# Summing eight of the modulation chunks of a conditioned conformer block on VectorE in SBUF

## The chip, the cores and the metric

The kernel runs on one core of a Trainium2 chip. The metric is the device time of one execution in microseconds (us). Three runs of the kernel before took 1474.2, 1476.01 and 1476.91 us, so the time before is the median, 1476.01 us. The trace shows the engines of the core: TensorE (PE, with its weight loads as PEld), VectorE (DVE), ScalarE (ACT), GpSimd (POOL) and SyncE (SP), which issues all the transfers of this stretch.

## What is computed

Two transformer-like blocks over 256 tokens of width 1024 (fp32). Only the start of the first block matters here:

```python
c_act = silu(c)                                  # (1, 1024)
mod = c_act @ mod_w + mod_b                      # (1, 6144): six rows of 1024
sh_m, sc_m, gt_m, sh_f, sc_f, gt_f = split(mod, 6)
h = rmsnorm(x, norm_pre_mix) * (1 + sc_m) + sh_m
u = h @ a_pw1_w + a_pw1_b                        # 1024 -> 2048
a, gt = split(u, 2);  u = a * sigmoid(gt)
u = causal_dwconv(u, dw_w) + dw_b                # 31 taps along the tokens
u = silu(layernorm(u, ln_g, ln_b))
y = u @ a_pw2_w + a_pw2_b
x = x + gt_m * rmsnorm(y, norm_post_mix)
```

The modulation row `mod` is a product of one vector of 1024 with a matrix of 1024 x 6144. The matrix is read in 24 chunks of 256 columns, 1 MB each.

## The kernel before

Every engine has its own program, in a fixed order written out by hand, and the engines wait for each other on semaphores. Large fp32 products are made of three products of rounded parts: a chunk of weights is loaded by SP into `a_raw` (two buffers), ScalarE writes its rounded high part (`split_hi`, L121), VectorE the remainder (`split_lo`, L125, which reads `a_raw` and the high part and writes the low part), and TensorE multiplies (L140 to L142). `split_lo` of a chunk also frees its `a_raw` buffer for the next load.

The stretch of the change is the first projection (`a_pw1_w`), eight steps j = 0 to 7, each over 128 channels. In step j the engines do this, in this order:

- TensorE: `project(j)` (48 matmuls for each of two halves of the work, in all L140 to L142), then from step 1 on `mod_sum` of the chunks of one unit of the modulation (L600), `mean(j-2)` (L907), `convolve(j-1)` (L899), and `mod_post(unit)` (L625 or L631).
- ScalarE: `split_hi(j+1)` (L121), the sigmoid (L799), `mod_take` of the unit's chunks (L609), its four of the sixteen shift copies (L789), `conv_out(j-1)` (L758).
- VectorE: `split_lo(j+1)` (L125), the gated product u (L1050), its six shift copies (L1054), then `mod_columns` (L642 to L645) or `mod_gate` (L654, L655) of the unit.
- GpSimd: the tap matrices of this step (L739, a product of two SBUF tensors, 128x1024; from step 2 on it waits for `convolve(j-2)`), its six shift copies (L745, L746) once u is there, and in step 5, behind its shift copies, the remainder of `mem` (L750, a difference of two SBUF tensors, 128x2048).

`convolve(j)` needs the tap matrices and the shift copies of all three engines; `project(j)` needs `split_lo` of its chunk and u of step j-2.

One chunk of the modulation goes through three pieces. `mod_sum` multiplies the chunk with silu(c) on TensorE: eight matmuls of 128x256 on 32 columns of the array each, four side by side, so that four partial sums stand in PSUM (in the trace 16 matmul records for a chunk). `mod_take` copies them to `modp` (two buffers) on ScalarE. `mod_post` adds the four partial sums in a second matmul with `sel`, a matrix with ones in four rows. Steps 1 to 4 take two chunks each (units 4 to 7: chunks 8 and 9, 10 and 11, 12 and 13, 14 and 15), steps 5 to 7 one each (units 8 to 10: chunks 16, 17, 18), and behind step 7 comes chunk 19 (unit 11), with `mean(6)`, `convolve(7)` and `mod_post(11)` behind it, and then the product of `mem` with its weights. The four slots for chunks are loaded by SP, in its fixed order among the other weights; the load of chunk i waits for `mod_used` of chunk i - 4.

Of the kernel before, what the change touches and what calls it, by code (L numbers as in the profile page):

```python
# [23 lines left out]
ALU = mybir.AluOpType  # L24
# [3 lines left out]
P = 128  # L28
# [185 lines left out]
def build_program(nc, A, out):  # L214
    with ExitStack() as ctx:
# [3 lines left out]
        def sem(name):  # L219
            return ctx.enter_context(nc.semaphore(name))  # L220
# [319 lines left out]

        def first_block():

            mods, u_pad, taps_w, shifted, conv, sq, sig, rstd, modp, stat32, sel, mask32, ones_mean = carve(
                (MOD_SLOTS, ACH), (2, PAD + SEQ + 2), (2, QUAD * TAPS), (2 * 4, SHIFT_LEN), (KD, SEQ), (KD, SEQ),
                (2, SEQ), (SEQ,), (2, MOD_COLS), (KD, QUAD), (P,), (QUAD,), (P,))
            hT = sq
            yb = shifted.rearrange("p a n -> p (a n)")[:, 0:NT * D].rearrange("p (t d) -> p t d", t=NT)
            xn = conv.rearrange("p k t -> p (k t)").rearrange("p (t d) -> p t d", t=NT)
# [12 lines left out]
            mod_loaded = [sem(f"mod_loaded{s}") for s in range(MOD_SLOTS)]  # L561
            mod_used, mod_taken, mod_posted, post_read = (sem(n) for n in ("mod_used", "mod_taken", "mod_posted",
                                                                         "post_read"))
            cond_ready, cond_sig = sem("cond_ready"), sem("cond_sig")
            xn_done, xn_turned = sem("xn_done"), sem("xn_turned")
            affine_done, input_done = sem("affine_done"), sem("input_done")
# [16 lines left out]
            def mod_bank(i):  # L583
                return 2 + i % 2 if i < 8 else (6, 3)[i % 2] if i < 20 else 4 + i % 2

            def post_bank(u):
                return 1 if u < 4 else 7

            def load_mod(sp, i):
                if i >= MOD_SLOTS:  # L590
                    sp.wait_ge(mod_used, i - MOD_SLOTS + 1)
                sp.dma_start(mods[:, i % MOD_SLOTS], A["mod_w"][MOD_ORDER[i]]).then_inc(mod_loaded[i % MOD_SLOTS], 16)

            def mod_sum(pe, i):

                pe.wait_ge(mod_loaded[i % MOD_SLOTS], 16 * (i // MOD_SLOTS + 1))
                if i >= 2:
                    pe.wait_ge(mod_taken, i - 1)
                for k in range(KD):
                    ins = pe.matmul(ps[quad[k % 4], mod_bank(i), 0:MOD_COLS], stat32[:, k],  # L600
                                    mods[:, i % MOD_SLOTS, k * MOD_COLS:(k + 1) * MOD_COLS], start=k < 4, stop=k >= 4)
                ins.then_inc(mod_used, 1)

            def mod_take(act, i):

                act.wait_ge(mod_used, i + 1)
                if i >= 2:
                    act.wait_ge(mod_posted, (i - 2) // 2 + 1 if i < 18 else i - 9)
                act.activation(modp[:, i % 2], ps[:, mod_bank(i), 0:MOD_COLS], ACT.Copy).then_inc(mod_taken, 1)  # L609

            def mod_copy(dve, i):

                dve.wait_ge(mod_used, i + 1)
                dve.wait_ge(mod_posted, i - 9)
                dve.tensor_copy(modp[:, i % 2], ps[:, mod_bank(i), 0:MOD_COLS]).then_inc(mod_taken, 1)

            def mod_post(pe, u):

                pe.wait_ge(mod_taken, unit_chunks(u)[-1] + 1)
                if 0 < u < 12:  # L620
                    pe.wait_ge(post_read, u)
                for s, i in enumerate(unit_chunks(u)):
                    if u < 8:
                        for h in range(2):
                            ins = pe.matmul(ps[:, post_bank(u), MOD_COLS + 2 * s + h:MOD_COLS + 2 * s + h + 1],  # L625
                                            modp[:, i % 2, h * P:(h + 1) * P], sel[:, 0:1], start=True, stop=True)
                    else:
                        c = u - 12
                        out_ = ps[:, 7, MOD_COLS:512] if u < 12 else \
                            ps[:, 6 + c // 2, (c % 2) * MOD_COLS:(c % 2 + 1) * MOD_COLS]  # L630
                        ins = pe.matmul(out_, sel, modp[:, i % 2], start=True, stop=True)  # L631
                ins.then_inc(mod_posted, 1)

            def mod_columns(dve, u):
# [31 lines left out]
            with nc.Block() as block:  # L666
# [46 lines left out]
                @block.gpsimd  # L713
                def _(pool):
                    pool_steps.step(pool, pool.memset(ident[:], 0.0))
                    pool_steps.step(pool, pool.affine_select(out=ident[:], in_=ident[:], compare_op=ALU.not_equal, fill=1.0,
                                                             base=0, pattern=[[-1, P]], channel_multiplier=1))
                    for i, v in enumerate((RMS_EPS, LN_EPS, LNX_EPS, 4 * LN_EPS)):
                        pool_steps.step(pool, pool.memset(eps[:, i:i + 1], v))
                    pool_steps.step(pool, pool.memset(stat32, 0.0))  # L720
                    pool_steps.step(pool, pool.memset(sel, 0.0))
                    for q in range(4):
                        pool_steps.step(pool, pool.memset(sel[q * QUAD:q * QUAD + 1], 1.0))
                        pool_steps.step(pool, pool.tensor_copy(mask32[quad[q]], ident[quad[q], quad[q]]))
                    pool_steps.step(pool, pool.memset(u_pad[:, :, 0:PAD], 0.0))
                    pool_steps.step(pool, pool.memset(u_pad[:, :, PAD + SEQ:PAD + SEQ + 2], 0.0))
                    pool_steps.step(pool, pool.memset(ones_mean, 1.0 / D))
                    pool_steps.step(pool, pool.memset(x_all[:, :, D:], 0.0))
                    pool_steps.step(pool, pool.memset(rows_all[:, :, D:], 0.0))
                    pool_steps.step(pool, pool.memset(head_ones[:], 0.0))  # L730
                    for h in range(2):
                        pool_steps.step(pool, pool.memset(head_ones[h * HD:(h + 1) * HD, h * HD:(h + 1) * HD], 1.0))
                    constants_at.append(pool_steps.n)
                    pool.wait_ge(rest_loaded, 16)
                    for j in range(KD):
                        if j >= 2:
                            pool.wait_ge(conv_pe, j - 1)
                        weights = cols("a_dw_t", TAPS * KD)[:, j * TAPS:(j + 1) * TAPS]
                        pool.tensor_tensor(taps[j % 2], mask32.unsqueeze(1).to_broadcast([P, TAPS, QUAD]),  # L739
                                           weights.unsqueeze(2).to_broadcast([P, TAPS, QUAD]),  # L740
                                           ALU.mult).then_inc(taps_made, 1)
                        pool.wait_ge(u_done, j + 1)
                        pool.wait_ge(taps_made, j + 1)
                        for q, a in SHIFTS_BY["pool"][:-1]:
                            pool_steps.step(pool, pool.tensor_copy(*shift_views(j, q, a)))  # L745
                        pool.tensor_copy(*shift_views(j, *SHIFTS_BY["pool"][-1])).then_inc(shift_pool, 1)  # L746
                        pool.wait_ge(shift_pool, j + 1)
                        if j == 5:
                            pool.wait_ge(mem_hi, 1)
                            pool.tensor_tensor(mem_parts[:, 1], mem_raw, mem_parts[:, 0].bitcast(F32),  # L750
                                               ALU.subtract).then_inc(mem_lo, 1)
# [3 lines left out]
                def _(act):  # L755
# [37 lines left out]
                    for j in range(KD):  # L793
# [6 lines left out]
                                       bias=col("a_pw1_b", KD + j)).then_inc(sig_done, 1)  # L800
                        if j:
                            for i in unit_chunks(PAIR_STEPS.get(j, GATE_STEPS.get(j))):
                                mod_take(act, i)
                        shifts(j)
                        if j:
                            conv_out(j - 1)
                    mod_take(act, unit_chunks(11)[0])
                    ring_a.split_hi(act, g_mem + 1)
                    conv_out(KD - 1)
                    for k in range(KD):  # L810
# [68 lines left out]
                def _(pe):  # L879
# [46 lines left out]
                    for j in range(1, KD):  # L926
# [4 lines left out]
                        project(j, 1, range(KD)).then_inc(ring_a.used, 1)  # L931
                        unit = PAIR_STEPS.get(j, GATE_STEPS.get(j))
                        for i in unit_chunks(unit):
                            mod_sum(pe, i)
                        if j >= 2:
                            mean(j - 2)
                        convolve(j - 1)
                        mod_post(pe, unit)
                    mod_sum(pe, unit_chunks(11)[0])
                    mean(KD - 2)  # L940
                    convolve(KD - 1)
                    mod_post(pe, 11)
# [73 lines left out]
                def _(dve):  # L1016
# [27 lines left out]
                    dve.wait_ge(rest_loaded, 16)  # L1044
                    for j in range(KD):
                        ring_a.split_lo(dve, g_pw1 + j + 1)
                        dve.wait_ge(sig_done, j + 1)
                        if j >= 2:
                            dve.wait_ge(conv_pe, j - 1)
# [6 lines left out]
                        if j in PAIR_STEPS:  # L1056
                            mod_columns(dve, PAIR_STEPS[j])
                        elif j in GATE_STEPS:
                            mod_gate(dve, GATE_STEPS[j])
                    ring_a.split_lo(dve, g_mem + 1)  # L1060
                    mod_gate(dve, 11)
                    dve.wait_ge(mean_pe, 1)
# [1954 lines left out]
```

## Time and profile before

| what | value |
|---|---|
| median of three runs | 1476.01 us (1474.2 to 1476.91) |
| the profiled execution's own time | 1475.35 us |
| its span in the trace | 1473.3 us |
| PE busy in the span | 1426.6 us, 97% |
| DVE busy | 952.4 us, 65% |
| ACT busy | 684.5 us, 46% |
| POOL busy | 157.6 us, 11% |

The span is what the trace covers; the execution's own time holds 2.05 us more. The busy shares are means over the whole kernel, and the stretch of the change is about 90 us of it. Matmuls overlap each other in the records, so the distance from one start to the next tells more of TensorE's time than the length of one.

### The profile page before, as it was taken

The numbers are of one execution on the slowest core, as the hardware profiler recorded it, in microseconds if no ns is written. First come the engines' busy times: TensorE is split into PE (matmuls) and PEld (weight loads), VectorE is DVE, ScalarE is ACT, GpSimd is POOL, SyncE is SP. The second block draws the span as 40 slices with busy tenths as digits, with TensorE's granted clock in tenths as the row PEclk, the third lists the DMA queues.
The fourth block names the chain that finished last, engine by engine and source line by source line (L and its number), as shares of the span: only waits on it lengthen the run. The fifth ranks groups of instructions, "written<-read, shape, count | busy, mean of one in ns | idle before, by whom it ended". The sixth has DMA issues, their size and how long they took to land.

```text
span 1473.3 us, 31313 instructions
## 1 busy us (share of the span) xinstructions
PE 1426.6 (97%) x12734; PEld 1298.2 (88%) x12734; DVE 952.4 (65%) x1284; ACT 684.5 (46%) x875; POOL 157.6 (11%) x179
## 2 busy tenths in 40 slices
PE   5999989999999999999999999999999999999997
PEld 3877779999899998998878999999999999899996
DVE  2656776666755556596677655676566678865656
ACT  3444554545533345754445334353343466534332
POOL 1342022232000002103300000000000012000000
PEclk8899999999999999999999999999999999999999
DMA  9975456666566665430127666656666444576662
GB/s 364 320 270 201 143 172 186 192 178 199 159 196 182 185 179 150 144 115 32 32 61 208 182 186 192 195 162 200 191 180 188 140 144 144 157 216 198 185 184 88
DMA packets 297973, 257.75 MB, mean 175 GB/s; under 512 B 7072, under 2 KB 274336, under 8 KB 294816
## 3 DMA queue, kind: packets, MB, share of 16 engines
q1 hardware_dynamic: 297888, 256.49, 57.3%
q8 instruction: 68, 1.11, 0.3%
q14 instruction: 17, 0.14, 0.0%
HBM read 255.42 MB, written 1.05 MB: 174 GB/s over the span
## 4 chain that ended last, share of the span: by engine, by line
PE 50%; DVE 4%; issue 1%; ACT 1%; DVEq 0%; ACTq 0%
PE ps L140 14%; PE ps L142 14%; PE ps L141 14%; PE ps L2228 3%; PE ps L372 1%; DVE stats L331 1%; DVE arena L329 1%; PE ps L379 1%; PE ps L458 0%; PE ps L463 0%; PE ps L459 0%; PE ps L2211 0%; PE ps L2219 0%; PE ps L2714 0%; DVE a_parts L2936 0%
## 5 line engine op out<-in xcount | busy, mean ns | idle before, releaser
L140 PE MATMUL ps<-actT,a_parts 128*128 128x256 f32 x2096 | 591.1, 282 | 7.0 <-DVE a_parts L1289 2.2
L141 PE MATMUL ps<-actT,a_parts 128*128 128x256 f32 x2096 | 587.7, 280 | 0.0
L142 PE MATMUL ps<-actT,a_parts 128*128 128x256 f32 x2096 | 587.1, 280 | 0.0
L140 PEld LDWEIGHTS ps<-actT,a_parts 128*128 128x128 f32 x2096 | 396.5, 189 | 16.3 <-issue 5.4
L141 PEld LDWEIGHTS ps<-actT,a_parts 128*128 128x128 f32 x2096 | 396.5, 189 | 4.2
L142 PEld LDWEIGHTS ps<-actT,a_parts 128*128 128x128 f32 x2096 | 396.6, 189 | 0.0
L1252 DVE TENSOR_TENSOR a_parts<-a_raw,a_parts 128x2048 fp32r<-128x2048 f32 x100 | 239.0, 2390 | 55.0 <-ACT a_parts L1249 54.7
L1266 DVE TENSOR_TENSOR b_parts<-b_raw,b_parts 128x1024 fp32r<-128x1024 f32 x72 | 88.2, 1225 | 160.5 <-ACT b_parts L1263 160.5
L1249 ACT ACTIVATE a_parts<-a_raw 128x2048 fp32r<-128x2048 f32 x100 | 190.3, 1903 | 0.0
L1263 ACT ACTIVATE b_parts<-b_raw 128x1024 fp32r<-128x1024 f32 x90 | 95.3, 1058 | 171.1 <-PE ps L142 171.1
L140 PE MATMUL ps<-b_parts,hid 128*128 128x512 f32 x400 | 158.1, 395 | 0.3 <-DVE hid L1363 0.3
L141 PE MATMUL ps<-b_parts,hid 128*128 128x512 f32 x400 | 158.3, 396 | 0.0
L142 PE MATMUL ps<-b_parts,hid 128*128 128x512 f32 x400 | 158.3, 396 | 0.0
L1311 ACT ACTIVATE arena<-ps 128x256 f32<-128x256 f32 x88 | 33.8, 384 | 241.9 <-PE ps L142 241.9
L125 DVE TENSOR_TENSOR a_parts<-a_raw,a_parts 128x2048 fp32r<-128x2048 f32 x37 | 87.5, 2364 | 28.7 <-ACT a_parts L121 28.6
L142 PEld LDWEIGHTS ps<-b_parts,hid 128*128 128x128 f32 x400 | 75.1, 188 | 18.2
L1357 DVE TENSOR_TENSOR arena<-arena,ps 128x256 f32<-128x256 f32 x88 | 37.1, 421 | 80.7 <-ACT arena L1311 80.7
L140 PEld LDWEIGHTS ps<-b_parts,hid 128*128 128x128 f32 x400 | 75.1, 188 | 14.4 <-issue 0.5
L141 PEld LDWEIGHTS ps<-b_parts,hid 128*128 128x128 f32 x400 | 75.1, 188 | 13.8
L121 ACT ACTIVATE a_parts<-a_raw 128x2048 fp32r<-128x2048 f32 x41 | 78.3, 1909 | 3.5 <-DMA a_raw<-in_rwkv_w_in 2.9
L1266 POOL TENSOR_TENSOR b_parts<-b_raw,b_parts 128x1024 fp32r<-128x1024 f32 x18 | 45.7, 2541 | 115.2 <-ACT b_parts L1263 115.2
L1363 DVE TENSOR_TENSOR hid<-arena,hid 128x256 fp32r<-128x256 f32 x110 | 46.8, 426 | 3.8
(381 smaller groups left out, 1819.6 us busy)
## 6 DMA issues: line engine op xcount, KB each, us to landing
a_raw<-in_ffn_w_gate SPq DMA_DIRECT2D x88, 512.0 KB, 4.0
a_raw<-in_ffn_w_up SPq DMA_DIRECT2D x88, 512.0 KB, 5.2
b_raw<-in_ffn_w_down SPq DMA_DIRECT2D x88, 512.0 KB, 3.3
arena<-in_mod_w SPq DMA_DIRECT2D x24, 1024.0 KB, 8.3
a_raw<-in_f_up_w SPq DMA_DIRECT2D x44, 512.0 KB, 5.0
b_raw<-in_f_down_w SPq DMA_DIRECT2D x22, 512.0 KB, 3.3
a_raw<-in_rwkv_w_in SPq DMA_DIRECT2D x10, 1024.0 KB, 5.3
a_raw<-in_sb_w_in SPq DMA_DIRECT2D x10, 1024.0 KB, 5.0
```

The costliest lines, as they stand in the source:

```text
L121: act.activation(self.parts[:, g % 2, 0], self.raw[:, g % 2], ACT.Copy).then_inc(self.hi_done, 1)
L125: dve.tensor_tensor(self.parts[:, g % 2, 1], self.raw[:, g % 2], self.parts[:, g % 2, 0].bitcast(F32), ALU.subtract).then_inc(self.lo_done, 1)
L140: pe.matmul(out, lhs[0], rhs[0], start=start, stop=False)
L141: pe.matmul(out, lhs[0], rhs[1], start=False, stop=False)
L142: return pe.matmul(out, lhs[1], rhs[0], start=False, stop=stop)
L1249: act.activation(a_parts[:, q, 0], a_raw[:, q], ACT.Copy).then_inc(ring_a.hi_done, 1)
L1252: dve.tensor_tensor(a_parts[:, q, 1], a_raw[:, q], a_parts[:, q, 0].bitcast(F32), ALU.subtract).then_inc(ring_a.lo_done, 1)
L1263: act.activation(b_of(q, j)[:, 0], b_raw[:, q], ACT.Copy).then_inc(ring_b.hi_done, 1)
L1266: lo.tensor_tensor(b_of(q, j)[:, 1], b_raw[:, q], b_of(q, j)[:, 0].bitcast(F32), ALU.subtract).then_inc(ring_b.lo_done, 1)
L1357: dve.tensor_tensor(hf[:, q], cg[:, q], up, ALU.mult).then_inc(f_step, 1)
L1363: dve.tensor_tensor(h_of(q, j)[:, 1], hf[:, q], h_of(q, j)[:, 0].bitcast(F32), ALU.subtract).then_inc(h_done, 1)
L2228: ins = pe.matmul(bank(b)[half[c], mm], lhs[half[c], p, mm], rhs[half[c], p, mm], start=True, stop=True)
```

## The change

Eight chunks, `ON_DVE` = 9, 11, 13, 15, 16, 17, 18 and 19, leave TensorE. For each of them VectorE makes `mod_add`: one `tensor_scalar` and seven `scalar_tensor_tensor` instructions of 128x256, each of which reads a slice of the chunk and the running total from SBUF and waits for the one before it. The total of each partition lands in `modp`, where `mod_take` had put the four partial sums; the 128 partitions are then added by the same `mod_post` matmuls, with a matrix of ones in place of `sel`. `mod_sum` and `mod_take` of these chunks are gone. In the VectorE program `mod_add` stands between `split_lo(j+1)` and u of step j, in steps 1 to 7 (chunks 9, 11, 13, 15, 16, 17, 18), and chunk 19's behind step 7, ahead of `split_lo` of the next chunk. `mod_post` waits for it, and so does the load that takes the same slot.

```diff
+            ON_DVE = [9, 11, 13, 15, 16, 17, 18, 19]
...
             def load_mod(sp, i):
                 if i >= MOD_SLOTS:
-                    sp.wait_ge(mod_used, i - MOD_SLOTS + 1)
+                    if i - MOD_SLOTS in ON_DVE:
+                        sp.wait_ge(mod_added, on_dve(i - MOD_SLOTS))
+                    else:
+                        sp.wait_ge(mod_used, on_pe(i - MOD_SLOTS))
...
+            def mod_add(dve, i):
+
+                dve.wait_ge(mod_loaded[i % MOD_SLOTS], 16 * (i // MOD_SLOTS + 1))
+                dve.wait_ge(mod_posted, (i - 2) // 2 + 1 if i < 18 else i - 9)
+                total = modp[:, i % 2]
+                for k in range(KD):
+                    rows_k = mods[:, i % MOD_SLOTS, k * MOD_COLS:(k + 1) * MOD_COLS]
+                    if k == 0:
+                        ins = dve.tensor_scalar(total, rows_k, csilu[:, 0:1], None, ALU.mult)
+                    else:
+                        ins = dve.scalar_tensor_tensor(total, rows_k, csilu[:, k:k + 1], total, ALU.mult, ALU.add)
+                    if k < KD - 1:
+                        dve_steps.step(dve, ins)
+                ins.then_inc(mod_added, 1)
...
             def mod_post(pe, u):
 
-                pe.wait_ge(mod_taken, unit_chunks(u)[-1] + 1)
+                last = unit_chunks(u)[-1]
+                pe.wait_ge(mod_taken, on_pe(last))
+                if last in ON_DVE:
+                    pe.wait_ge(mod_added, on_dve(last))
...
-                        ins = pe.matmul(out_, sel, modp[:, i % 2], start=True, stop=True)
+                        ins = pe.matmul(out_, ones if i in ON_DVE else sel, modp[:, i % 2], start=True, stop=True)
...
                         for i in unit_chunks(unit):
-                            mod_sum(pe, i)
+                            if i not in ON_DVE:
+                                mod_sum(pe, i)
                         if j >= 2:
                             mean(j - 2)
                         convolve(j - 1)
                         mod_post(pe, unit)
-                    mod_sum(pe, unit_chunks(11)[0])
                     mean(KD - 2)
...
                         ring_a.split_lo(dve, g_pw1 + j + 1)
+                        if j:
+                            mod_add(dve, unit_chunks(PAIR_STEPS.get(j, GATE_STEPS.get(j)))[-1])
                         dve.wait_ge(sig_done, j + 1)
...
+                    mod_add(dve, unit_chunks(11)[0])
                     ring_a.split_lo(dve, g_mem + 1)
```

One more memset of 128x128 (`ones`) stands among GpSimd's constants at the start.

## Rows read from the trace of the kernel before

**Rows 1.** The page: busy time, share and instructions of each engine

```profile
PE 1426.6 (97%) x12734; PEld 1298.2 (88%) x12734; DVE 952.4 (65%) x1284; ACT 684.5 (46%) x875; POOL 157.6 (11%) x179
```

**Rows 2.** Timeline of PE, the stretch: start us, duration us, instruction, count

```profile
56.47 1.05 PE L625 MATMUL ps<-arena 128*128 128x1 f32 x8
...
88.71 1.93 PE L600 MATMUL ps<-arena 128*32 128x256 f32 x32
90.58 0.70 PE L907 MATMUL ps<-arena 128*128 128x256 f32 x2
...
101.49 1.07 PE L600 MATMUL ps<-arena 128*32 128x256 f32 x16
102.49 0.70 PE L907 MATMUL ps<-arena 128*128 128x256 f32 x2
...
112.94 1.07 PE L600 MATMUL ps<-arena 128*32 128x256 f32 x16
...
135.47 0.70 PE L631 MATMUL ps<-arena 128*128 128x256 f32 x2
```

**Rows 3.** Timeline of DVE, the same stretch

```profile
50.40 3.36 DVE L125 TENSOR_TENSOR a_parts<-a_raw,a_parts 128x2048 fp32r<-128x2048 f32 x1 [1.11 <-ACT a_parts L121]
53.68 0.47 DVE L1050 SCALAR_TENSOR_TENSOR arena<-ps,par,arena 128x256 f32<-128x256 f32 x1
...
71.69 2.29 DVE L125 TENSOR_TENSOR a_parts<-a_raw,a_parts 128x2048 fp32r<-128x2048 f32 x1 [0.27 <-ACT a_parts L121]
...
102.62 2.65 DVE L1054 COPY arena<-arena 32x284 f32<-32x284 f32 x6
107.45 0.42 DVE L654 TENSOR_TENSOR gate_m<-ps,gate_m 128x256 f32<-128x256 f32 x1 [2.17 <-PE ps L631]
107.91 2.65 DVE L655 TENSOR_TENSOR gate_m<-gate_m,rows 128x256 f32<-128x256 f32 x1
110.48 4.00 DVE L125 TENSOR_TENSOR a_parts<-a_raw,a_parts 128x2048 fp32r<-128x2048 f32 x1
```

**Rows 4.** Timeline of POOL, the same stretch

```profile
49.69 1.91 POOL L739 TENSOR_TENSOR arena<-arena,par 128x1024 f32<-128x1024 f32 x1
...
102.65 2.46 POOL L745 COPY arena<-arena 32x284 f32<-32x284 f32 x5 [5.69 <-DVE arena L1050]
105.18 0.42 POOL L746 COPY arena<-arena 32x284 f32<-32x284 f32 x1
105.68 4.60 POOL L750 TENSOR_TENSOR b_parts<-b_raw,b_parts 128x2048 fp32r<-128x2048 f32 x1
110.24 2.10 POOL L739 TENSOR_TENSOR arena<-arena,par 128x1024 f32<-128x1024 f32 x1
```

**Rows 5.** Timeline of ACT, step 5

```profile
103.03 1.79 ACT L789 ACTIVATE arena<-arena 32x284 f32<-32x284 f32 x4
...
107.22 1.91 ACT L121 ACTIVATE a_parts<-a_raw 128x2048 fp32r<-128x2048 f32 x1
```

**Rows 6.** Groups of DVE by shape, whole span: busy us, mean ns, idle before

```profile
L354 DVE TENSOR_SCALAR x_tok<-arena,stats 128x512 f32<-128x512 f32 x10 | 5.4, 543 | 0.0
...
L2057 DVE SCALAR_TENSOR_TENSOR arena<-arena,par 128x256 f32<-128x256 f32 x6 | 2.5, 478 | 0.0
...
L1030 DVE TENSOR_SCALAR arena<-x_tok,stats 128x1024 f32<-128x1024 f32 x2 | 1.5, 754 | 0.1
```

**Rows 7.** Timeline of PE after the first block, with its idle time

```profile
195.28 0.39 PE L140 MATMUL ps<-actT,a_parts 128*128 128x256 f32 x1 [1.90 <-DVE a_parts L1289]
...
206.86 0.39 PE L140 MATMUL ps<-actT,a_parts 128*128 128x256 f32 x1 [1.87 <-DVE a_parts L1252]
```

**Rows 8.** Windows of PE: busy us, records, granted clock, DMA share, GB/s

```profile
197.00:198.00 1.00, 1.00 (x11) 1.00 0.05 16
...
208.00:209.00 1.00, 1.00 (x7) 0.55 0.62 169
...
211.00:212.00 1.00, 1.00 (x8) 0.74 0.80 193
```

More of the change, by code:

```diff
@@ L541, in first_block @@
         def first_block():
-            mods, u_pad, taps_w, shifted, conv, sq, sig, rstd, modp, stat32, sel, mask32, ones_mean = carve(
+            mods, u_pad, taps_w, shifted, conv, sq, sig, rstd, modp, stat32, sel, mask32, ones_mean, ones = carve(
                 (MOD_SLOTS, ACH), (2, PAD + SEQ + 2), (2, QUAD * TAPS), (2 * 4, SHIFT_LEN), (KD, SEQ), (KD, SEQ),
-                (2, SEQ), (SEQ,), (2, MOD_COLS), (KD, QUAD), (P,), (QUAD,), (P,))
+                (2, SEQ), (SEQ,), (2, MOD_COLS), (KD, QUAD), (P,), (QUAD,), (P,), (P,))
             hT = sq
@@ L563, in first_block @@
                                                                          "post_read"))
+            mod_added = sem("mod_added")
             cond_ready, cond_sig = sem("cond_ready"), sem("cond_sig")
@@ L584, in mod_bank, with on_dve, on_pe @@
                 return 2 + i % 2 if i < 8 else (6, 3)[i % 2] if i < 20 else 4 + i % 2
+            ON_DVE = [9, 11, 13, 15, 16, 17, 18, 19]
+            def on_dve(i):
+                return sum(1 for v in ON_DVE if v <= i)
+            def on_pe(i):
+                return i + 1 - on_dve(i)
             def post_bank(u):
@@ L597, in mod_sum @@
                 if i >= 2:
-                    pe.wait_ge(mod_taken, i - 1)
+                    pe.wait_ge(mod_taken, on_pe(i - 1) - (i < 9))
                 for k in range(KD):
@@ L604, in mod_take @@
             def mod_take(act, i):
-                act.wait_ge(mod_used, i + 1)
+                act.wait_ge(mod_used, on_pe(i))
                 if i >= 2:
@@ L609, in mod_take @@
                 act.activation(modp[:, i % 2], ps[:, mod_bank(i), 0:MOD_COLS], ACT.Copy).then_inc(mod_taken, 1)
+            def mod_add(dve, i):
[11 more added lines that the diff above has]
+                ins.then_inc(mod_added, 1)
             def mod_copy(dve, i):
-                dve.wait_ge(mod_used, i + 1)
+                dve.wait_ge(mod_used, on_pe(i))
                 dve.wait_ge(mod_posted, i - 9)
@@ L625, in mod_post @@
                             ins = pe.matmul(ps[:, post_bank(u), MOD_COLS + 2 * s + h:MOD_COLS + 2 * s + h + 1],
-                                            modp[:, i % 2, h * P:(h + 1) * P], sel[:, 0:1], start=True, stop=True)
+                                            modp[:, i % 2, h * P:(h + 1) * P],
+                                            (ones if i in ON_DVE else sel)[:, 0:1], start=True, stop=True)
                     else:
@@ L727, in _ @@
                     pool_steps.step(pool, pool.memset(ones_mean, 1.0 / D))
+                    pool_steps.step(pool, pool.memset(ones, 1.0))
                     pool_steps.step(pool, pool.memset(x_all[:, :, D:], 0.0))
@@ L802, in _ @@
                             for i in unit_chunks(PAIR_STEPS.get(j, GATE_STEPS.get(j))):
-                                mod_take(act, i)
+                                if i not in ON_DVE:
+                                    mod_take(act, i)
                         shifts(j)
@@ L806, in _ @@
                             conv_out(j - 1)
-                    mod_take(act, unit_chunks(11)[0])
                     ring_a.split_hi(act, g_mem + 1)
@@ L933, in _ @@
                         for i in unit_chunks(unit):
-                            mod_sum(pe, i)
+                            if i not in ON_DVE:
+                                mod_sum(pe, i)
                         if j >= 2:
```

## Prediction

> **What bounds the kernel now.** I read the page first: TensorE is busy 97% of the span [rows 1], so a microsecond taken from its order of work is worth one, as long as nothing else is late. Then the timelines of the four engines over the first projection, 50 to 142 us. TensorE goes through the steps without idle time: step 4's block starts at 88.71, step 5's at 101.49 and step 6's at 112.94, so a step with two chunks takes 12.78 us and one with a single chunk 11.45 [rows 2]. VectorE, ScalarE and GpSimd have idle time in each step; VectorE spends some 7 of the 12 us. Of VectorE's rows the reader is to see two that are far too long: the split L125 takes 2.29 us when it is alone, but 3.36 at 50.40 and 4.00 at 110.48, and L655 takes 2.65 us at 107.91 [rows 3], though its neighbour L654, of the same shape, takes 0.42. GpSimd's rows say why. L739 runs from 49.69 to 51.60, L750 from 105.68 to 110.28 and L739 again from 110.24 to 112.34 [rows 4], and each long VectorE row ends behind one of them: L655 at 110.56, just behind L750; L125 at 53.76 and 114.48, each 2.15 us behind the end of L739. So a VectorE instruction with both inputs in SBUF stands still while GpSimd runs a product or difference of two SBUF tensors, and loses all of that time but the 0.14 us of its own start-up. L654 ran beside L750 without loss: one of its inputs is in PSUM. `mod_add` and L125 both have the shape that stands still.
>
> **What the change takes from TensorE.** The two chunks of step 4 take 1.87 us up to the next instruction, the single one of step 5 takes 1.00 [rows 2], so one of two is worth 0.87 and a single one 1.00. Four of each kind go: 4 x 0.87 + 4 x 1.00 = 7.5 us. ScalarE loses eight copies of under half a microsecond, which waited for TensorE anyway and are worth nothing. The extra memset is among constants that are made before TensorE's first work: nothing.
>
> **What it adds to VectorE.** `scalar_tensor_tensor` of 128x256 from SBUF takes 0.478 us (L2057) [rows 6]. Each waits for the one before; from L654 to L655, which wait in the same way at 107.45, the distance is 0.46 us for a row of 0.42 [rows 3], so 0.04 more: 0.518 each. The first, a `tensor_scalar` of 128x256, isn't in the trace. The nearest are 0.754 us for 128x1024 and 0.543 for 128x512 [rows 6]; the straight line through them gives 0.44 at 256 columns, and a quarter of the longer one, 0.19, is the bound below. I take 0.36, nearer the line, and 0.40 with its wait. A chunk is then 0.40 + 6 x 0.518 + 0.478 = 3.99 us to its signal, and 3.91 until VectorE's next instruction can start. Bounds for a dependent instruction: 0.44 us, if start-up and wait overlap more than in these rows, and 0.56, if each wait costs twice what it costs there. Here the Trainium skill (VectorE: DVE Perf Modes, section on Mode 2x_2P) says that an fp32 `tensor_scalar` from SBUF runs at two elements a cycle because it uses both read ports for one tensor; with the page's 0.96 GHz that is an estimate of 0.13 us behind a start-up, which no row here separates, and eight chunks would come out up to 0.7 us shorter in all.
>
> **Where these 4 us land.** They stand between `split_lo` and the product u. The work that has hidden so much of VectorE's stretch is TensorE's step; what matters is VectorE's own circle from u to u. GpSimd begins its shift copies 0.55 us after u starts; from their start (102.65) to what follows on GpSimd (105.68) it is 3.03 us [rows 4], then comes L739 with 1.91. Before, GpSimd reached L739 only when TensorE's `convolve` was over; now u is late, the convolution is long done and L739 follows the copies directly. The split wants to start in this time: ScalarE's shift copies (1.79), a short eviction and its half of the split (1.91) [rows 5] are over some 4.5 us after u, before L739 ends at 5.5. So the split waits for L739, and VectorE is free 2.08 us after L739's end (51.60 to 53.68) [rows 3, 4]. Then `mod_add`. The circle is 0.55 + 3.03 + 1.91 + 2.08 + 3.91 = 11.5 us.
>
> TensorE's circle with the chunk gone is 12.78 - 0.87 = 11.9 us up to step 4, but 11.45 - 1.00 = 10.45 from step 5 on. So VectorE is just fast enough in the first half and too slow in the second. In order:
>
> - Step 1. VectorE is free at 53.68 [rows 3], `mod_add(9)` signals at 57.7. TensorE wants it for `mod_post` at 56.47 - 0.87 = 55.6 [rows 2]: it waits 2.1 us. u starts at 57.6.
> - Steps 2 to 5. u starts at 69.1, 80.6, 92.0 and 103.5; TensorE, 11.9 us a step from 57.7, reaches its `mod_post` at 69.6, 81.5, 93.4 and, after a short step, 104.3. The sums are there 0.4 to 1.3 us earlier. No wait, the saving is kept: TensorE is 4 x 0.87 + 1.00 - 2.1 = 2.4 us ahead of before.
> - Step 6. In step 5 GpSimd has L750 too, 4.60 us, and it can start as soon as its copies are over: u + 3.6 = 107.1. L655 or the split stands still until it ends, and then L739 gets its turn (2.10, as at 110.24) [rows 4]. This was so before as well, but there were 3 us of slack; now the sum stands behind it. u of step 6 starts at 103.5 + 11.5 + 4.6 + 0.1 = 119.7, and `mod_add(17)` signals at 119.8. TensorE wants it at 104.3 + 10.45 = 114.8: it waits 5.0 us. Whether L655 or L750 comes first changes nothing, since both precede the sum.
> - Step 7. u at 131.2; TensorE wants the sum at 119.8 + 10.45 = 130.3, and waits 1.0 us.
> - Chunk 19. Behind u come shift copies and gate: 0.52 + 2.58 + 0.81, then the sum, which signals at 131.2 + 3.9 + 4.0 = 139.1. TensorE waits meanwhile for `conv_out(6)`, which ScalarE has behind the late u, and for the shift copies; its `convolve(7)` is over at 138.3. `mod_post(11)` starts at 139.15, where it was 135.47 before [rows 2]: 3.7 us later.
>
> So 7.5 us saved, and waits of 2.1 + 5.0 + 1.0 + 3.1 = 11.2 us in their place. Behind `mod_post(11)` both TensorE and VectorE are late by about the same, and TensorE is busy almost throughout to the end, so nothing gives it back.
>
> **SP's queue.** The loads of chunks 13, 15, 17, 19 and 20 to 23 now wait for VectorE. The latest against before is chunk 13, from some 53 to 57.7 us, and everything behind it in SP's order with it, the weights of step 4 above all; ScalarE wants those at about 71.6, and issue to landing is below 10 us. The loads behind chunk 19 are late by 8 us, for use at the end of the block, 35 us later. I cost the queue at nothing; with this cover gone it would be at most the 4 us of delay, once.
>
> **The clock.** After an idle spell of 1.87 us before 206.86 the granted clock was half, the lower of its two levels, from the window 208 to 209 (0.55) to 211 to 212 (0.74), some 3.4 us; after one of 1.90 before 195.28 it stayed whole [rows 7, 8]. 3.4 us at half rate lose 1.7 us of work. The wait of 5.0 us should bring such a spell; of its 1.7 us, 1.0 goes into the wait of step 7, so it costs 0.7. The four waits of the tail may bring another, with nothing to cover it, and that of step 1 one that the slack of VectorE's circle mostly swallows.
>
> **Sum.** 3.7 + 0.7 = +4.4 us on the profiled execution's 1475.35 (span 1473.3 and 2.05 around it): 1479.8. The median of the runs is 0.66 above that execution, so 1480.4 us.
>
> **Rivals.** A: this chain, 1480.4, from 1478 to 1483 by its own terms; chance 0.57. B: the clock falls more than once and costs in the tail, 1.7 us each for two more spells: 1483.8; for it that the tail has four waits in 9 us, against it that one idle spell of 1.9 us did nothing; 0.15. C: L750 stays out of the circle, because VectorE's instructions get in between or GpSimd starts it late: without its 4.6 us the circle gives -0.6 us and 1475.4, no difference; against it stands L655's row; 0.18. A dependent instruction of 0.44 us in place of 0.518 makes eight chunks 3.7 us shorter and ends near the same, +0.0; 0.56, with 0.45 for the first, makes them 2.4 us longer and gives +6. D, the other side: GpSimd's operations hold up neither the splits nor the sums. VectorE's circle is then 4.5 + 2.2 + 3.9 = 10.6 us, TensorE waits only at step 1 (2.1) and 0.5 us in the last steps: 7.5 - 2.6 = 4.9 gained, 1471.1 us. It decides from the point where VectorE's circle is shorter than TensorE's 10.45; for it speaks only that L739 might fall beside the product u, whose first input is in PSUM; 0.10. The Trainium skill (SBUF — State Buffer, section Who interferes with whom) has it that VectorE and GpSimd share one pair of ports as an exclusive lock that whoever starts first holds for the whole instruction; by that rule D is out, and so far the trace agrees with it (2.65 us for L655).
>
> **Chances and range.** About 0.2%, 2.95 us, is what a measurement of this kernel can tell from no change. Slower by more (above 1478.96): most of A, 0.48, and B, 0.15: 0.63. Within: the rest of A, 0.09, and C, 0.18: 0.27. Faster: D, 0.10. The range leaves out D and the far end of B: 1475.2 to 1484.0. The likeliest case alone: 1478 to 1483.
>
> **What would show it.** `scalar_tensor_tensor` rows of 0.48 at distances of 0.52, eight a chunk in 4.0 us; L1050 every 11.5 us up to step 5 and 16 us from step 5 to 6; TensorE idle 2 us before L625 near 57.7 and 5 us before L631 near 119.8, released by VectorE; L750 at about 107 with L655 or L125 as long; `mod_post(11)` near 139 us; everything behind it shifted by the same. Wrong would make it: shorter sums, L750 beside work that it doesn't hold up, a transfer that is waited for in the steps, or half clock over long parts of the tail.

## The result, and the profile after

The changed kernel takes 1480.45 us (median of six runs, 1479.42 to 1481.77), the kernel before 1475.11 in six runs. The ratio is 1.0039, with a 95% interval of 1.0028 to 1.0050: 5.8 us slower, from 4.1 to 7.4. The forecast was 1480.4, 4.4 us slower.

In the new kernel's line numbers `mod_sum` is L612, `mod_post` L655 and L662, `mean` L939, `convolve` L931, u L1084, the gate L685 and L686; GpSimd's tap matrices are L771 and its mem operation L782; `mod_add` is L631 (first instruction) and L633. First the page's line that answers to [rows 1]: TensorE has 7 us less work (1426.6 before) in a span of 1478.0 us, which is 4.7 longer.

```profile
PE 1419.4 (96%) x12606; PEld 1295.7 (88%) x12606; DVE 985.4 (67%) x1348; ACT 682.0 (46%) x867; POOL 157.6 (11%) x180
```

The groups of VectorE by shape in the stretch (busy us, mean ns, idle before) have the two new instructions, 0.485 and 0.342 us each:

```profile
L633 DVE SCALAR_TENSOR_TENSOR arena<-arena,small 128x256 f32<-128x256 f32 x56 | 27.2, 485 | 2.0
L631 DVE TENSOR_SCALAR arena<-arena,small 128x256 f32<-128x256 f32 x8 | 2.7, 342 | 0.0
```

VectorE's timeline after, to be read beside [rows 3]:

```profile
44.12 0.49 DVE L1084 SCALAR_TENSOR_TENSOR arena<-ps,par,arena 128x256 f32<-128x256 f32 x1 [3.75 <-ACT arena L831]
...
55.60 0.48 DVE L1084 SCALAR_TENSOR_TENSOR arena<-ps,par,arena 128x256 f32<-128x256 f32 x1
...
101.50 0.48 DVE L1084 SCALAR_TENSOR_TENSOR arena<-ps,par,arena 128x256 f32<-128x256 f32 x1
...
105.17 4.80 DVE L686 TENSOR_TENSOR gate_m<-gate_m,rows 128x256 f32<-128x256 f32 x1
109.89 3.99 DVE L125 TENSOR_TENSOR a_parts<-a_raw,a_parts 128x2048 fp32r<-128x2048 f32 x1
113.80 0.34 DVE L631 TENSOR_SCALAR arena<-arena,small 128x256 f32<-128x256 f32 x1
114.18 3.61 DVE L633 SCALAR_TENSOR_TENSOR arena<-arena,small 128x256 f32<-128x256 f32 x7
117.70 0.48 DVE L1084 SCALAR_TENSOR_TENSOR arena<-ps,par,arena 128x256 f32<-128x256 f32 x1
...
121.38 2.10 DVE L686 TENSOR_TENSOR gate_m<-gate_m,rows 128x256 f32<-128x256 f32 x1
...
129.50 0.48 DVE L1084 SCALAR_TENSOR_TENSOR arena<-ps,par,arena 128x256 f32<-128x256 f32 x1
```

GpSimd's timeline beside it, for [rows 4]:

```profile
105.08 4.60 POOL L782 TENSOR_TENSOR b_parts<-b_raw,b_parts 128x2048 fp32r<-128x2048 f32 x1
109.63 2.10 POOL L771 TENSOR_TENSOR arena<-arena,par 128x1024 f32<-128x1024 f32 x1
...
121.29 1.91 POOL L771 TENSOR_TENSOR arena<-arena,par 128x1024 f32<-128x1024 f32 x1
```

From u of step 1 (55.60) to u of step 2 (67.07) it is 11.47 us, and to u of step 5 (101.50) 45.90, four times 11.475. Then L782 and L771 pass, L686 and L125 stand still beside them, and u of step 6 is 16.20 us later. TensorE's timeline, with its idle time before a row in brackets, for [rows 2]:

```profile
55.78 1.02 PE L655 MATMUL ps<-arena 128*128 128x1 f32 x8 [2.00 <-issue]
...
117.89 1.19 PE L662 MATMUL ps<-arena 128*128 128x256 f32 x2 [5.31 <-issue]
...
130.92 0.70 PE L662 MATMUL ps<-arena 128*128 128x256 f32 x2
...
132.35 0.70 PE L939 MATMUL ps<-arena 128*128 128x256 f32 x2 [0.73 <-ACT arena L790]
...
137.61 0.67 PE L662 MATMUL ps<-arena 128*128 128x256 f32 x2 [0.80 <-issue]
...
179.39 1.07 PE L612 MATMUL ps<-arena 128*32 128x256 f32 x16
181.96 1.07 PE L612 MATMUL ps<-arena 128*32 128x256 f32 x16 [1.50 <-ACT arena L621]
...
187.20 1.07 PE L612 MATMUL ps<-arena 128*32 128x256 f32 x16 [1.28 <-DVE arena L642]
...
191.97 3.98 PE L437 MATMUL ps<-actT,a_parts 128*128 128x256 f32 x32 [1.80 <-PEq L697]
```

The reader is to see the waits of 2.0 and 5.3 us where they were forecast, and two that were not: 1.50 and 1.28 us between the sums of the last four chunks, which stay on TensorE. They have nothing to do with VectorE. The changed `mod_sum` of chunk i waits for `on_pe(i - 1)` copies, where `on_pe(i)` counts the chunks up to i that stay on TensorE. For the even chunks of the steps, whose odd neighbour is on VectorE, that is the copy of chunk i - 2, as before, but for chunks 21 to 23 it is the copy of chunk i - 1. The prediction's account of the change passes over this line.

One more thing is needed to compare. In the profiled execution of before, u of step 0 starts at 46.11 us (the row below is from its VectorE timeline), after at 44.12. So I measure from u of step 0.

```profile
46.11 0.48 DVE L1050 SCALAR_TENSOR_TENSOR arena<-ps,par,arena 128x256 f32<-128x256 f32 x1 [3.41 <-ACT arena L799]
```

| from u of step 0 | to `mod_post(11)` | against before | to L437, the next block's first products | against before |
|---|---|---|---|---|
| before | 89.36 | | 141.38 | |
| after | 93.49 | +4.1 | 147.85 | +6.5 |

The rows of TensorE in before that the last column rests on, from the first sum of the last four chunks to L437:

```profile
177.28 1.93 PE L600 MATMUL ps<-arena 128*32 128x256 f32 x32
...
187.49 4.01 PE L437 MATMUL ps<-actT,a_parts 128*128 128x256 f32 x32 [1.80 <-PEq L666]
```

Since u of step 0 starts 2.0 us earlier in the profile after, the two spans differ by only 4.7 us, though the part behind it is 6.5 us longer.

### The profile page after: what moved, and what is told of

It reads as the page before. It is cut to its first block, busy times and chain, and to the rows that moved or that the text cites. A ratio compares the mean times of both kernels' runs of the same rounds, so it can differ in the third digit from the quotient of the medians.

```text
span 1478.0 us, 31106 instructions
## 1 busy us (share of the span) xinstructions
PE 1419.4 (96%) x12606; PEld 1295.7 (88%) x12606; DVE 985.4 (67%) x1348; ACT 682.0 (46%) x867; POOL 157.6 (11%) x180
## 4 chain that ended last, share of the span: by engine, by line
PE 50%; DVE 4%; ACT 0%; issue 0%; DVEq 0%; ACTq 0%
PE ps L140 14%; PE ps L142 13%; PE ps L141 13%; PE ps L2263 3%; PE ps L372 1%; DVE stats L331 1%; DVE arena L329 1%; PE ps L379 1%; PE ps L458 0%; PE ps L463 0%; PE ps L459 0%; PE ps L2246 0%; PE ps L2254 0%; DVE gate_m L2566 0%; DVE a_parts L2971 0%
## 5 line engine op out<-in xcount | busy, mean ns | idle before, releaser
L125 DVE TENSOR_TENSOR a_parts<-a_raw,a_parts 128x2048 fp32r<-128x2048 f32 x37 | 90.3, 2442 | 29.0 <-ACT a_parts L121 28.9
```

What stands on the lines that cost most here:

```text
L125: dve.tensor_tensor(self.parts[:, g % 2, 1], self.raw[:, g % 2], self.parts[:, g % 2, 0].bitcast(F32), ALU.subtract).then_inc(self.lo_done, 1)
```

## The experiments

**One wait as it was.** In this and all later variants of the changed kernel:

```diff
-                    pe.wait_ge(mod_taken, on_pe(i - 1) - (i < 9))
+                    pe.wait_ge(mod_taken, on_pe(i - 2))
```

> The changed kernel with one wait as it was before: TensorE's sum of chunk i waits for the copy of chunk i - 2 and no longer, from chunk 21 on, for that of chunk i - 1. Theory T (the circle of VectorE costs about 4 us up to the product of mem, and the stricter wait costs another 2.4 us in the four last chunks, where the profile after shows TensorE idle for 1.5 and 1.28 us): from the first of these four sums to the next block's first products 10.2 us in place of 12.6, the rest as in the changed kernel, so 2.4 us less than it, about 1478. Rival R (the idle time there is only moved, since the turned tokens wait for VectorE anyway): the stretch stays within 0.5 us of 12.6 and the time at 1480.5.

Measured: 1476.98 us against 1474.24, ratio 1.0029 (1.0016 to 1.0043), 2.4 to 6.3 us slower than before. TensorE's timeline of this run:

```profile
179.52 1.93 PE L612 MATMUL ps<-arena 128*32 128x256 f32 x32
...
183.27 1.93 PE L612 MATMUL ps<-arena 128*32 128x256 f32 x32
...
189.74 3.98 PE L437 MATMUL ps<-actT,a_parts 128*128 128x256 f32 x32 [1.80 <-PEq L697]
```

Both pairs of sums run through without idle time, and from the first to L437 it is 10.22 us, as in the kernel before (177.28 to 187.49, 10.21), in place of 12.58. From u of step 0 (44.12) to `mod_post(11)` (137.73) it is 93.61 us. So by the traces the moved sums cost 4.2 us and the wait 2.4. R falls. (By the runs alone the two kernels aren't told apart: the interval here, 2.4 to 6.3, overlaps the 4.1 to 7.4 of the changed kernel. The next run carries the 2.4.)

**That wait alone, in the kernel before.**

```diff
-                    pe.wait_ge(mod_taken, i - 1)
+                    pe.wait_ge(mod_taken, i - 1 + (i >= 21))
```

> The kernel before with the stricter wait alone: TensorE's sum of chunks 21, 22 and 23 waits for the copy of the chunk just before it. Theory T: idle times of about 1.5 and 1.3 us between these sums, 12.6 us from the first of them to the next block's first products in place of 10.2, so 2.4 us more than the kernel before: 1476.7 against 1474.3. Rival R (in the kernel before, VectorE and the copies are late there in another order, so the wait is hidden): no change. Beside it: the start of u of step 0, at 46.1 us in the profile before and at 43.8 to 44.1 in the five since; if that is chance of the clock in one execution it comes near 44 here too, although nothing of the first 170 us is changed.

Measured: 1477.11 against 1474.67, ratio 1.0016 (1.0007 to 1.0026), 2.4 us slower (1.0 to 3.8). The rows of VectorE (u of step 0) and of TensorE:

```profile
44.31 0.48 DVE L1050 SCALAR_TENSOR_TENSOR arena<-ps,par,arena 128x256 f32<-128x256 f32 x1 [3.72 <-ACT arena L799]
```

```profile
175.41 1.07 PE L600 MATMUL ps<-arena 128*32 128x256 f32 x16
177.99 1.07 PE L600 MATMUL ps<-arena 128*32 128x256 f32 x16 [1.50 <-ACT arena L609]
...
183.23 1.07 PE L600 MATMUL ps<-arena 128*32 128x256 f32 x16 [1.28 <-DVE arena L615]
...
188.00 4.01 PE L437 MATMUL ps<-actT,a_parts 128*128 128x256 f32 x32 [1.80 <-PEq L666]
```

The same two waits, 12.59 us to L437. And u of step 0 comes at 44.3 with code that is the old one up to there, so the 46.1 of the first profile was chance and no part of the change (it is 43.8 to 44.3 in the other runs, and 45.2 in the copy variant below). The windows show where it arose: in the first profile the granted clock is half in every window from 28 to 44 us, in this run and after the change it is whole from 32 to 38. The two waits add up to 2.8 us, but the stretch is only 2.4 longer; a wait of 0.77 us for VectorE, which TensorE has there in the kernel before (at 183.73), is gone.

**The mem operation without its reads.** GpSimd's operation of step 5:

```diff
-                            pool.tensor_tensor(mem_parts[:, 1], mem_raw, mem_parts[:, 0].bitcast(F32),
-                                               ALU.subtract).then_inc(mem_lo, 1)
+                            pool.memset(mem_parts[:, 1].bitcast(F32), 0.0).then_inc(mem_lo, 1)
```

> As e1_chunk_wait, but GpSimd's remainder of mem (128x2048, 4.60 us) is a memset of the same tile, which reads no SBUF: the low part of mem is left out as zeros. Theory T (VectorE's circle holds this operation in full, because it stands still beside it): the instruction of gate_m in step 5 takes 0.4 in place of 4.80 us, u of step 6 follows that of step 5 after about 12 us in place of 16.2 (if the memset is short), and mod_post(11) is 4.4 us earlier, measured from u of step 1: 77.6 in place of 82.0. Rival R1 (it is the length of the GpSimd operation in its own order that counts, not the port): with a memset of some 2 us, u to u is 14 us. Rival R2 (lock against any GpSimd operation that touches SBUF): the gate_m instruction is as long as the memset.

Measured: one run, 1475.67 us. VectorE's and GpSimd's timelines (u is L1083 in this variant):

```profile
101.16 0.48 DVE L1083 SCALAR_TENSOR_TENSOR arena<-ps,par,arena 128x256 f32<-128x256 f32 x1
...
104.81 0.42 DVE L686 TENSOR_TENSOR gate_m<-gate_m,rows 128x256 f32<-128x256 f32 x1
105.79 2.29 DVE L125 TENSOR_TENSOR a_parts<-a_raw,a_parts 128x2048 fp32r<-128x2048 f32 x1 [0.56 <-ACT a_parts L121]
108.00 2.00 DVE L631 TENSOR_SCALAR arena<-arena,small 128x256 f32<-128x256 f32 x1
110.04 3.61 DVE L633 SCALAR_TENSOR_TENSOR arena<-arena,small 128x256 f32<-128x256 f32 x7
113.57 0.48 DVE L1083 SCALAR_TENSOR_TENSOR arena<-ps,par,arena 128x256 f32<-128x256 f32 x1
```

```profile
104.70 1.82 POOL L782 MEMSET b_parts<- 128x2048 f32 x1
106.59 3.26 POOL L771 TENSOR_TENSOR arena<-arena,par 128x1024 f32<-128x1024 f32 x1
```

L686 takes 0.42 us inside the memset: R2 falls, and with 12.41 us from u to u R1 (14) too. The rows also show the order turned round. L125 starts before L771, and now L771 waits for it (3.26 us in place of 1.91), and then L631, the first instruction of the sum, stands still beside L771 (2.00 us in place of 0.34). The sum of chunk 19 ends at 133.35, 78.0 us after u of step 1, in place of 81.9: 3.9 us earlier, where 4.4 were expected. TensorE got less of it. `mod_post(11)` starts only at 135.02, 91.2 us after u of step 0, 2.3 us earlier than after the change, because TensorE ran at half clock there: it had waited 1.50 us before 125.55 and 1.99 us before 128.21, and the granted clock was half from 127 to some 133.6. TensorE's windows of this run (length and busy us, records, granted clock, DMA share, GB/s):

```profile
128.00:129.00 1.00, 0.79 (x2) 0.50 0.91 360
...
133.00:134.00 1.00, 1.00 (x17) 0.70 0.75 303
```

**The mem operation as a copy.** In the same place:

```diff
+                            pool.tensor_copy(mem_parts[:, 1], mem_raw).then_inc(mem_lo, 1)
```

> As e1_chunk_wait, but GpSimd's remainder of mem is a copy of mem, 128x2048, with one SBUF input in place of two: the low part of mem is left out and its rounded value stands there instead. Theory T1 (a VectorE instruction with two SBUF inputs stands still beside any GpSimd operation that reads SBUF, as the Trainium skill has it): the gate_m instruction of step 5 takes as long as the copy (some 2 to 4 us), u to u of step 6 is 11.5 us plus that length. Rival T2 (only GpSimd's two-input products hold it): the gate_m instruction takes 0.42 us and u to u is 12.4, as with the memset.

Measured: one run, 1476.98 us. VectorE's and GpSimd's rows:

```profile
106.20 2.08 DVE L686 TENSOR_TENSOR gate_m<-gate_m,rows 128x256 f32<-128x256 f32 x1
```

```profile
106.10 1.90 POOL L782 CAST b_parts<-b_raw 128x2048 fp32r<-128x2048 f32 x1
```

L686 stands still until the copy is over, and u to u is 13.48 us (102.55 to 116.03), 11.5 plus the copy's 1.9. In this variant GpSimd's operation is called CAST, and it is as long as the memset (1.82). A single input of GpSimd in SBUF is enough: T1 holds, as the Trainium skill states it (SBUF — State Buffer, section Who interferes with whom), T2 falls. So of these three operations it is the reading, not the length, that holds VectorE's two-input instruction.

**Only the first four chunks.**

```diff
-            ON_DVE = [9, 11, 13, 15, 16, 17, 18, 19]
+            ON_DVE = [9, 11, 13, 15]
...
+                    mod_take(act, unit_chunks(11)[0])
...
+                    mod_sum(pe, unit_chunks(11)[0])
...
-                        if j:
+                        if j and unit_chunks(PAIR_STEPS.get(j, GATE_STEPS.get(j)))[-1] in ON_DVE:
...
-                    mod_add(dve, unit_chunks(11)[0])
```

> As e1_chunk_wait, but only chunks 9, 11, 13 and 15 (steps 1 to 4, where each step keeps another chunk on TensorE) are summed by VectorE; 16 to 19 are back on TensorE. Theory T (VectorE's circle of 11.5 us fits under TensorE's 11.9 there; only step 1 waits): TensorE idle 2.0 us before mod_post of step 1 and nowhere else in the steps, mod_post(11) 1.5 us earlier than in the kernel before, measured from project(1): a gain of 1.5 us, 1473.6 against 1475.1. Rival R (the sums cost as such, by their port or by the late u, wherever they stand): no gain, or a loss of about 2 us.

Measured: 1474.05 against 1474.24, ratio 1.0001 (0.9992 to 1.0010). In the trace TensorE waits once for a sum:

```profile
55.71 1.02 PE L655 MATMUL ps<-arena 128*128 128x1 f32 x8 [2.15 <-issue]
```

The three others cost it no wait, and `mod_post(11)` starts at 132.14, 88.08 us after u of step 0 (44.06): 1.3 us earlier than before. The runs don't show these 1.3 us; their interval ends at a gain of 1.2. So the expectation of 1.5 us holds in the trace alone, and by the runs the "no gain" of R isn't excluded. Its "loss of about 2 us" is; the interval ends at a loss of 1.5.

**Only the last four.** The list is another one, and chunk 19 stays with VectorE (`mod_add` behind step 7, no `mod_sum`):

```diff
+            ON_DVE = [16, 17, 18, 19]
```

> As e1_chunk_wait, but only chunks 16 to 19 (steps 5 to 7 and behind) are summed by VectorE; 9, 11, 13 and 15 are back on TensorE. Theory T (here a step of TensorE is 10.45 us, shorter than VectorE's circle of 11.5, and the 4.60 us of GpSimd's mem operation stand in the circle): these four lose all that the changed kernel loses: mod_post(11) about 4.0 us later than before, measured from u of step 0 (93.4 against 89.4), TensorE idle 3.5 us before mod_post of step 6; the time 1478.3 against 1474.3. Rival R (the first four, with the wait of 2.1 us at step 1, carry the loss, and the last four gain what they take from TensorE): mod_post(11) 4 us earlier.

Measured: 1477.14 against 1474.67, ratio 1.0018 (1.0008 to 1.0027), 1.2 to 4.0 us slower. TensorE's rows:

```profile
117.39 1.19 PE L662 MATMUL ps<-arena 128*128 128x256 f32 x2 [3.92 <-issue]
...
137.09 0.67 PE L662 MATMUL ps<-arena 128*128 128x256 f32 x2 [0.80 <-issue]
```

`mod_post(11)` at 93.29 us after u of step 0 (43.80), 3.9 later than before: nearly all of the 4.1 that the changed kernel loses. R falls. The parts don't add up (-1.3 for the first four, +3.9 for these, +4.1 or 4.2 for all), and the rows say why: from u of step 5 to `mod_post(11)` it is 36.1 us here (100.99 to 137.09) and after the change (101.50 to 137.61), so from there VectorE sets the pace, and what the first four save on TensorE before is lost in its wait.

**The four that fit.** The edits of the first four, with another list:

```diff
+            ON_DVE = [11, 13, 15, 18]
```

> As e1_chunk_wait, but chunks 11, 13, 15 and 18 alone are summed by VectorE: those whose step has slack on VectorE. Theory T: no wait of TensorE for a sum at all, 3 x 0.87 + 1.00 = 3.6 us gained against the kernel before, so 1471.5 against 1475.1, and the fastest of all. Rival R (as above): no gain. In the profile: TensorE's rows without idle time before L655 and L662 in steps 1 to 7.

Measured: 1469.42 against 1474.24, ratio 0.9967 (0.9956 to 0.9977), 3.4 to 6.5 us faster than the kernel before. R falls. No row of TensorE for a sum or a `mod_post` in this stretch has idle time before it; the last is

```profile
129.32 0.70 PE L662 MATMUL ps<-arena 128*128 128x256 f32 x2
```

From u of step 0 (43.77) to `mod_post(11)` it is 85.55 us, 3.8 us less than before, where 3.6 were expected. This version beats both kernels.

**The sum behind u.** All eight on VectorE, but in another place:

```diff
                         ring_a.split_lo(dve, g_pw1 + j + 1)
-                        if j:
-                            mod_add(dve, unit_chunks(PAIR_STEPS.get(j, GATE_STEPS.get(j)))[-1])
...
                         ins.then_inc(shift_dve, 1)
+                        if j:
+                            mod_add(dve, unit_chunks(PAIR_STEPS.get(j, GATE_STEPS.get(j)))[-1])
```

> As e1_chunk_wait, all eight chunks on VectorE, but in steps 1 to 7 the sum stands behind u and VectorE's shift copies, ahead of the work on the unit's columns. Theory T: u is no longer late, but the sum begins 3.7 us after TensorE's project and takes 4.0, so TensorE waits for it at mod_post in every step, 2 us in steps 1 to 4 and 3 in 5 to 7, and 1.9 more where GpSimd's tap matrices fall into the sum: mod_post(11) 10 to 15 us later than before and some 1485 to 1490 us. Rival R (it is the late u that costs, by what GpSimd and ScalarE do behind it): faster than e1_chunk_wait, below 1477.

Measured: 1518.58 us (two runs) against 1474.67, ratio 1.0293 (1.0272 to 1.0314), 40 to 46 us slower than before. TensorE's rows and windows:

```profile
60.34 1.84 PE L655 MATMUL ps<-arena 128*128 128x1 f32 x8 [7.01 <-issue]
...
79.24 1.26 PE L655 MATMUL ps<-arena 128*128 128x1 f32 x8 [4.24 <-issue]
...
138.28 1.19 PE L662 MATMUL ps<-arena 128*128 128x256 f32 x2 [9.63 <-issue]
```

```profile
80.00:82.00 2.00, 2.00 (x10) 0.50 0.80 254
82.00:84.00 2.00, 2.00 (x14) 0.68 0.97 361
```

The wait of step 2 is 4.24 us, what T has with GpSimd's 1.9, and so are those of steps 3 and 4. Those of the steps 1, 5, 6 and 7 are longer than T has them: 7.01, 9.63, 5.59 and 3.91 us. In step 5 the seven `scalar_tensor_tensor` take 9.33 us in place of 3.61, since GpSimd's mem operation (128.74, 4.50 us) and its tap matrices (133.20, 2.08 us) run beside them. And after each wait the granted clock is half for some microseconds of `project`, as in these windows; u waits for `project`, so nothing covers it: from u of step 2 (70.33) to that of step 3 (88.12) it is 17.8 us, 11.9 + 4.2 + 1.7. T had the direction and the wait, and a third of the size at most. `mod_post(11)` is 133.53 us after u of step 0, 44.2 later than before, and the sum is this: 38.9 us of waits, where T has 17 and 1.9 for each tap product that falls into a sum; less the 7.5 saved; and a rest of 12.8 us, an estimate of what the half clock costs, which T left out. R falls.

## Why the prediction was right, and where it was not

**TensorE's saving, 7.5 us.** Right where nothing waits: of the four that fit, three of 0.87 and one of 1.00 give 3.6, measured 3.8.

**The length of a sum.** 3.99 us to the signal were forecast; 0.38 + 3.61 = 3.99 measured (113.80 to 117.79). `tensor_scalar` takes 0.342, `scalar_tensor_tensor` 0.485; the 0.36 taken for the first was close, and the straight line through the longer shapes (0.44) was too high. From 0.342 at 256 columns to 0.754 at 1024 it is 0.54 ns a column; the two elements a cycle of the Trainium skill (VectorE: DVE Perf Modes, section on Mode 2x_2P), with the page's 0.96 GHz, give an estimate of 0.52. The trace agrees with the page in these two rows; the 0.543 at 512 columns lies above the line between them.

**VectorE's circle.** 11.5 us forecast, 11.47 measured, and 16.2 from step 5 to 6, forecast 16.2. From step 6 to 7 it is 11.80 (117.70 to 129.50), 0.3 more: L686 too stands still beside L771 (121.38, 2.10 us) and has to finish before L125, a term that the prediction left out.

**TensorE's waits.** Forecast 2.1, 5.0, 1.0 and 3.1 in the tail; measured 2.0, 5.3, none, and 1.5 in the tail (0.73 and 0.80). That the last two are shorter is the clock, not a gain (below). The whole, to `mod_post(11)`: forecast +3.7, measured +4.1 and +4.2.

**The clock, +0.7.** The spell came, behind the wait of 5.3 us, and longer than forecast: half from 118 to 124, some 6.5 us in place of 3.4. TensorE's windows after the change (length and busy us, records, granted clock, DMA share, GB/s):

```profile
116.00:117.00 1.00, 0.00 (x0) 1.00 1.08 386
...
118.00:119.00 1.00, 1.00 (x3) 0.50 0.31 95
...
124.00:125.00 1.00, 1.00 (x10) 1.00 0.00 0
```

`project(7)` takes 8.3 us up to `mean` (118.52 to 126.81) in place of some 5.9. But it cost nothing: VectorE set the pace, and TensorE only waited less for it in step 7 and the tail. The variant with the old wait bears this out. Its spell in step 7 is shorter (windows 118 to 122), TensorE waits 2.7 us in the tail in place of 1.5, and `mod_post(11)` comes at the same place (93.61 against 93.49). There a spell behind step 1's wait (half clock in the windows 57 to 60) likewise left u of step 2 where it was (67.03 against 67.07). The term of 0.7 is mis-sized: for this chain it measured about zero. Rival B, more spells with a price in the tail, did not come in this execution; in the variant with the memset it did, and took 1.6 us.

**Behind `mod_post(11)`.** That nothing gives the delay back there held. But the prediction has no term for this part at all, and this is the step that failed: the stricter wait of the last chunks adds 2.4 us, shown alone in the kernel before. TensorE works in order, so the sum of chunk 21 can't start before the copy of chunk 20 is over, and TensorE stands still for the copy (the 1.50 us behind ScalarE's L621, and the 1.28 us behind VectorE's L642).

**The sum.** By the traces the parts are 4.1 (forecast 3.7), 0 (0.7) and 2.4 (none): 6.5 in place of 4.4. The median of before came out 0.9 lower in six runs than in three, so that 1480.45 falls on 1480.4 is partly luck: against the traces the forecast has 0.4 too little up to `mod_post(11)`, 0.7 too much for the clock and 2.4 too little behind it, and it starts from a time that is 0.9 higher. Both sums lie in the measured interval of 4.1 to 7.4 us.

**The rivals.** C (L750 outside the circle, no difference) and D (no holding up, faster) are out by the rows of 4.80 and 3.99 us; the memset shows what C's premise would be worth, 3.9 us of VectorE's time. (C's -0.6 us should be about -1.0 by the prediction's own steps: u of step 6 at 115.0, waits of 2.1, 0.3, 1.0 and 3.1 us against 7.5 saved. Nothing hangs on it.) SP's queue cost nothing: no row of TensorE or VectorE in the steps waits for a transfer.

## What to carry to other kernels

Work moved from the busiest engine to one that looks idle is paid by the circle of the engine that takes it, from one of its results to the next, with all that other engines do in between; compare that circle with the step of the busy engine, stage by stage, and move only what fits. Here (11.5 us against 11.9 and 10.45) four of eight pieces fit and gain 3.8 us, and the other four turn that into a loss of 4.2. When a wait is rewritten for a new numbering, check it for every index, also for the pieces that don't move: a single count too many for three of them cost 2.4 us, more than half of the 4.2 that the moved work lost.

## What the runs showed of the hardware

A VectorE instruction with two SBUF inputs stands still beside a GpSimd product or difference that reads SBUF (4.80 us in place of 0.42), and even beside a copy with a single input (2.08), but not beside a memset (0.42). The fp32 `tensor_scalar`, with one SBUF tensor, did so too (2.00 us in place of 0.34 beside the tap product). Whoever starts first goes through: GpSimd's product took 3.26 us in place of 1.91 when VectorE's L125 had begun 0.8 us before it. Half-clock spells behind a wait of TensorE cost nothing where another engine set the pace (the 8.3 us of `project(7)`), and were paid in full where that engine in turn waited for TensorE (1.7 us of the 17.8 us from u to u in the sum behind u).
